# The second pair of a recursive up-projection made classical, its operand differences moved to later pairs

## The chip, the cores and the metric

The kernel runs on 1 core of a Trainium2 chip. The metric is the device time of one execution in microseconds. Times inside an execution are read from one profiled execution and count from the start of its span.

## The reference

One decoder block over 2048 tokens of 1024 channels, in float32. The part that the change touches is the gated MLP:

```
v    = rms_norm(h, g_ffn)
up   = causal_dwconv(v @ w_up, w_conv_ffn, b_conv_ffn)      # 1024 -> 2 x 3072, three taps
gate, val = up[..., :3072], up[..., 3072:]
h    = h + (gelu(gate) * val) @ w_down                      # 3072 -> 1024
```

Ahead of it stand an input projection with a linear recurrence and a causal pooling, and an output projection; behind it a gated per-layer embedding (`w_ple_gate`, `w_ple_proj`) and a last RMS norm.

## The kernel before

Everything is stored channel-major: a tile is 128 channels on the partitions by tokens. The tokens are done in two blocks of 1024, one after the other, each through all stages: mixing, output projection, eight products of the embedding (`pp`), the MLP, the gate of the embedding.

**Precision.** A float32 operand is split in two parts, hi = the rounded value and lo = the remainder, and a product of two such operands is three matmuls: hi x hi, hi x lo, lo x hi. Weights come in panels of 4 tiles of 128x128 (`raw`, a ring of 5 buffers, loaded by SP's queue). ScalarE writes the panel's hi part (`hi(n)`, L627), VectorE the lo part (`lo(n)`, L1069), in rings of 4 (`whi`, `wlo`). `hi(n)` waits until TensorE has used panel n - 4, and for TensorE a panel is ready when `lo(n)` is done. A raw buffer is loaded again when its last panel's `lo` is done.

**The MLP.** The 3072 channels of gate and val are 24 tiles each. Tile q of gate and tile q of val are a pair. Pair 0 of each block is done classically: 8 input tiles, each times gate's and val's weights, times two halves of 512 tokens, times three = 96 matmuls, with gate and val interleaved tile by tile, as the input's splits become ready. Every other pair is one level of Strassen's recursion in Winograd's form: the pair's 2x2 matrix of (gate, val) x (lower, upper half of the input channels) times the input's 2x2 matrix of (channel halves) x (token halves) takes seven products P1 to P7 of 12 matmuls, 84 in all. Its left operands are four panels as they are or sums of panels, which VectorE forms afresh in each pair (`wsummed`, L1065, one buffer). Its right operands are the input's quarters B11, B12, B21, B22 and four differences T1 to T4. They are formed once a block by VectorE (L1321, 128x2048), in place in the input `UN`, and split by ScalarE (L804) and VectorE (L1326). T4's split parts overwrite those of B12.

The products run in the order P1 P5 P6 P3 P7 P2 P4. Between them ScalarE copies partial results out (`snap_p1` after P1, `snap_p5`, `snap_u2`), and VectorE adds others (`c12_out` after P3, `c22_out` after P7, `c11_out` after P2). P6 waits for `snap_p1`, P3 for `snap_p5`, P7 for `snap_u2` and P4 for `c22_out`. In the first recursive pair P5, P6, P7 and P4 also wait for T1, T2, T3 and T4.

Each finished pair is convolved: for gate and for val one ScalarE pass (`gate_sum`, `val_sum`) and two chained VectorE passes (`gate_conv`, `val_conv`), then gelu (ScalarE), a product (`f_tile`) and its split into `f_split` (`f_hi_tile`, `f_lo_tile`). Four pairs make a chunk of f, and after each chunk come the 8 down products (192 matmuls). Results leave in four PSUM slots used in turn.

Each engine's program is a list written out by hand, and an engine works through it strictly in that order; engines meet only in semaphores. For the opening of the stage there are own lists, `first_pair` and `second_pair` on ScalarE and VectorE; from then on `pair(b, q)` is repeated. In `first_pair` the embedding's products are also brought out (`keep_pp`) and the input is normalised and split (`normalised`, `b_hi_tile`, `b_lo_tile`).

Of the kernel before, what the change touches and what calls it, by code (L numbers as in the profile page):

```python
# [36 lines left out]
AHEAD_DOWN = 3  # L37

# [6 lines left out]
PRODUCTS = (("P1", B11), ("P5", T1), ("P6", T2), ("P3", B22), ("P7", T3), ("P2", B21), ("P4", T4))  # L45
OP_AT = {B11: 4, B12: 5, B21: 1, B22: 2, T1: 3, T2: 0, T3: 6, T4: 5}
# [8 lines left out]
def plan():  # L55
# [46 lines left out]
    for b in range(BLOCKS):  # L102
# [83 lines left out]
PAIRS = FT - 1  # L186
# [35 lines left out]
def build(nc, xT, pT, wpan, par_d, outT, pp_d):  # L222
    with ExitStack() as ctx:
# [34 lines left out]
        f_split = place("f_split", [P, 2, CHUNK, BLOCK], F32R, F0)  # L258
# [82 lines left out]
        def landed(r):  # L341
            return panel_in[r % RAW_RING], 16 * (r // RAW_RING + 1)

# [92 lines left out]
        def _(pe):  # L436
# [62 lines left out]
            def first_pair(b):  # L499
                gate, val = (b, "gate", 0), (b, "val", 0)  # L500
                pe.wait_ge(*free(gate))
                pe.wait_ge(*free(val))
                for k in range(DT):
# [7 lines left out]
                    if k % KP == KP - 1:  # L511
                        mm.then_inc(pe_step, 1)
# [13 lines left out]
            def pair(b, q):  # L526
                xy, z = (b, "XY", q), (b, "Z", q)
                s = b * PAIRS + q - 1
                X, Y, Z = psum(xy)[:, 0:BANK], psum(xy)[:, BANK:BLOCK], psum(z)[:, 0:BANK]

                def t_formed(i):
                    if q == 1:
                        pe.wait_ge(t_ready, b * 4 + i)
# [4 lines left out]
                t_formed(1)  # L538
                product(b, q, "P5", T1, Z, True)
                pe.wait_ge(snapped, 3 * s + 1)  # L540
                t_formed(2)
# [4 lines left out]
                t_formed(3)  # L546
# [3 lines left out]
                t_formed(4)  # L550
                product(b, q, "P4", T4, X, False)

            def down(b, c, m, k0, k1):
# [5 lines left out]
                for k in range(k0, k1):  # L559
                    pe.wait_ge(f_ready, b * FT + c * CHUNK + k + 1)  # L560
                    mm = tile_products(psum(key), n, k,
                                       lambda part, h, k=k: f_split[:, part, k, h * BANK:(h + 1) * BANK],
# [5 lines left out]
            for b in range(BLOCKS):  # L568
# [23 lines left out]
                for c in range(CHUNKS):  # L592
                    for q in range(c * CHUNK, (c + 1) * CHUNK):
                        if q == 0:
                            first_pair(b)
                        else:
                            pair(b, q)
# [21 lines left out]
        def _(act):  # L619
# [181 lines left out]
            def t_hi_half(b, i, name):  # L801
                act.wait_ge(t_sum, b * 4 + i)
                half = {T1: (0, 0), T3: (0, 1), T2: (1, 1), T4: (1, 0)}[name]
                nc.scalar.activation(op_half(name, 0), un_half(*half), ACT.Copy).then_inc(t_hi, 1)  # L804
# [9 lines left out]
            def gate_sum(b, q):  # L814
                if q:
                    act.wait_ge(*out_of((b, "Z", q)))
                    act.wait_ge(c11, b * PAIRS + q)
# [807 lines left out]
```

## Time and profile before

| | us |
|---|---|
| median of 3 runs | 2225.94 (2224.36 to 2226.24) |
| the profiled execution | 2225.44 |
| its span, first to last instruction | 2223.7 |
| TensorE busy | 2159.3 (97%) |
| VectorE busy | 1545.0 (69%) |
| ScalarE busy | 1025.2 (46%) |
| mean granted TensorE clock | 0.990 |

A granted clock of 1.00 is 2.4 GHz and 0.50 is 1.2 GHz. The difference between the profiled execution's time and its span, 1.7 us, lies outside the first and the last instruction. In the timeline rows one row may merge several instructions of a kind (x2, x4); a row's duration is longer than the distance from its start to the next start, as instructions of an engine overlap at their ends.

### The profile page before, as it was taken

What the parts mean: (1) busy time and instruction counts of PE and PEld (TensorE: products, weight loads), DVE (VectorE), ACT (ScalarE), POOL (GpSimd) and SP (SyncE); (2) the same over time, 40 slices, a digit from 0 to 9 for tenths busy, and PEclk for the clock granted to TensorE, in tenths of its full rate; (3) what the DMA queues carried; (4) which work ended last, traced back from release to release, by engine and by line L of the source; (5) the groups of instructions that cost most, each with busy time, mean ns of one, the idle gap of its engine ahead of it and who ended that gap; (6) DMA issues with size and microseconds to landing.
All of it is one profiled execution on the core that took longest, in us unless ns stands there. A gap on an engine that the chain in (4) does not pass through costs nothing.

```text
span 2223.7 us, 24264 instructions
## 1 busy us (share of the span) xinstructions
PE 2159.3 (97%) x9416; PEld 1775.3 (80%) x9416; DVE 1545.0 (69%) x1769; ACT 1025.2 (46%) x1403; POOL 0.2 (0%) x4
## 2 busy tenths in 40 slices
PE   8999989999999999999999999899999999999995
PEld 6877868888888888888888788688888888888884
DVE  7884497585858575777888736967667575848765
ACT  5763455352525253454555625534334352525443
POOL 0000000000000000000000000000000000000000
PEclk9999999999999999999999999999999999999998
DMA  3114211121211111133221233111211121211222
GB/s 142 51 43 152 95 57 57 41 73 38 67 40 54 50 57 57 51 134 106 70 114 50 71 126 114 38 57 43 72 38 63 43 66 38 72 43 53 71 100 76
DMA packets 73154, 154.81 MB, mean 70 GB/s; under 512 B 7888, under 2 KB 8016, under 8 KB 73040
## 3 DMA queue, kind: packets, MB, share of 16 engines
q1 hardware_dynamic: 70736, 144.87, 19.4%
q10 hardware_dynamic: 2304, 8.39, 0.9%
q8 instruction: 75, 1.23, 0.2%
q14 instruction: 39, 0.32, 0.0%
HBM read 136.45 MB, written 16.78 MB: 69 GB/s over the span
## 4 chain that ended last, share of the span: by engine, by line
PE 90%; DVE 6%; ACT 2%; issue 1%; DMA 0%; SPq 0%; ACTq 0%; DVEq 0%
PE slot L448 51%; PE slot L521 38%; DVE wlo L1069 1%; DVE UN L1309 1%; DVE ops L1314 1%; DVE UN L1321 1%; DVE H L1538 0%; DMA XN<-xT 0%; DVE H L1268 0%; PE slot L477 0%; ACT ops L804 0%; DVE ops L1326 0%; ACT whi L627 0%; DVE H L1264 0%; DVE H L1274 0%
## 5 line engine op out<-in xcount | busy, mean ns | idle before, releaser
L521 PE MATMUL slot<-ops,whi 128*128 128x512 f32 x2576 | 799.2, 392 | 19.3 <-ACT WG L853 9.9
L521 PEld LDWEIGHTS slot<-ops,whi 128*128 128x128 f32 x2576 | 486.5, 189 | 123.4 <-ACT WG L853 10.7
L521 PE MATMUL slot<-ops,wlo 128*128 128x512 f32 x1288 | 503.5, 391 | 0.0
L627 ACT ACTIVATE whi<-raw 128x512 fp32r<-128x512 f32 x370 | 229.1, 625 | 469.1 <-PE slot L448 312.1
L448 PE MATMUL slot<-f_split,whi 128*128 128x512 f32 x1536 | 410.5, 389 | 0.0
L448 PEld LDWEIGHTS slot<-f_split,whi 128*128 128x128 f32 x1536 | 288.4, 188 | 59.8
L1069 DVE TENSOR_TENSOR wlo<-raw,whi 128x512 fp32r<-128x512 f32 x370 | 249.5, 687 | 60.8 <-ACT whi L627 60.0
L521 PEld LDWEIGHTS slot<-ops,wlo 128*128 128x128 f32 x1288 | 243.3, 189 | 50.9
L627 ACT ACTIVATE whi<-wsum 128x512 fp32r<-128x512 f32 x184 | 115.6, 628 | 322.7 <-DVE wsum L1065 191.9
L1463 DVE TENSOR_TENSOR H<-slot,H 128x1024 f32<-128x1024 f32 x96 | 117.3, 1222 | 182.1 <-PE slot L448 182.1
L448 PE MATMUL slot<-f_split,wlo 128*128 128x512 f32 x768 | 236.4, 389 | 0.0
L448 PE MATMUL slot<-Uhi,whi 128*128 128x512 f32 x640 | 202.4, 398 | 17.6 <-DVE wlo L1069 16.9
L448 PE MATMUL slot<-Ulo,whi 128*128 128x512 f32 x640 | 198.5, 392 | 0.0
L448 PE MATMUL slot<-Uhi,wlo 128*128 128x512 f32 x640 | 198.5, 392 | 0.0
L448 PEld LDWEIGHTS slot<-f_split,wlo 128*128 128x128 f32 x768 | 144.2, 188 | 29.9
L1069 DVE TENSOR_TENSOR wlo<-wsum,whi 128x512 fp32r<-128x512 f32 x184 | 126.8, 689 | 51.2 <-ACT whi L627 51.2
L448 PEld LDWEIGHTS slot<-Uhi,whi 128*128 128x128 f32 x640 | 120.9, 190 | 46.9 <-issue 15.5
L448 PEld LDWEIGHTS slot<-Ulo,whi 128*128 128x128 f32 x640 | 121.4, 190 | 25.7
L448 PEld LDWEIGHTS slot<-Uhi,wlo 128*128 128x128 f32 x640 | 121.0, 189 | 25.3
L448 PE MATMUL slot<-Yhi,whi 128*128 128x512 f32 x304 | 93.9, 390 | 3.4 <-DVE Ylo L1278 3.4
L448 PE MATMUL slot<-Yhi,wlo 128*128 128x512 f32 x304 | 93.6, 389 | 0.0
L448 PE MATMUL slot<-Ylo,whi 128*128 128x512 f32 x304 | 93.5, 389 | 0.0
(176 smaller groups left out, 2222.9 us busy)
## 6 DMA issues: line engine op xcount, KB each, us to landing
raw<-panels SPq DMA_DIRECT2D x416, 256.0 KB, 2.7
XN<-xT SPq DMA_DIRECT2D x8, 1024.0 KB, 9.0
H<-xT SPq DMA_DIRECT2D x8, 1024.0 KB, 11.0
pp_kept<-XQ ACTq DMA_DIRECT2D x16, 512.0 KB, 2.6
PPR<-pp_kept SPq DMA_DIRECT2D x16, 512.0 KB, 3.5
outT<-H SPq DMA_DIRECT2D x8, 512.0 KB, 2.7
outT<-H SPq DMA_DIRECT2D x16, 256.0 KB, 2.4
WG<-pT SPq DMA_DIRECT2D x2, 512.0 KB, 9.1
```

The lines of the kernel that those rows point to most:

```text
L448: mm = pe.matmul(ps[:, h * BANK:(h + 1) * BANK], stat_[:, w], mov(part, h), start=first and i == 0, stop=last and i == 2)
L521: mm = pe.matmul(ps, stat_[:, w], (lo if part else hi)[:, k, :], start=first and k == 0 and i == 0, stop=k == KP - 1 and i == 2, skip_grou ...
L627: nc.scalar.activation(whi[n % RING][:], source(n), ACT.Copy).then_inc(panel_hi, 1)
L1069: v.tensor_tensor(wlo[n % RING][:], source(n), f32(whi[n % RING][:]), ALU.subtract).then_inc(panel_lo, 1)
L1309: v.scalar_tensor_tensor(UN[:, k, :], H[:, k, :], col("g_ffn", k), rms_tile(1), ALU.mult, ALU.mult).then_inc(un_ready, 1)
L1314: v.tensor_tensor(b_tile(k, 1), halves(UN[:, k, :]), f32(b_tile(k, 0)), ALU.subtract).then_inc(b_ready, 1)
L1321: v.tensor_tensor(un_half(*dst), un_half(*left), un_half(*right), ALU.subtract).then_inc(t_sum, 1)
L1463: v.tensor_tensor(H[:, m, :], psum(key)[:], H[:, m, :], ALU.add).then_inc(slot_free[SLOT[key]], 1)
```

## The change

Pair 1 of each block is done classically as well, so 22 instead of 23 pairs a block are recursive, and the first recursive pair is pair 2. In pair 1 all of gate (48 matmuls) comes ahead of all of val (48). The four differences are formed in the order T1, T3, T2, T4: T1 and T3 on VectorE behind the last splits of the input, T2 during pair 1, T4 during pair 2, once B12 is no longer used. Their splits, the convolutions and the panels of pairs 0 to 2 stand in new lists (`second_pair`, `third_pair`). `keep_pp(6)`, `keep_pp(7)` and the panel c0 + 3 come a place or two earlier in `first_pair`. `f_split` is laid out tile by tile, so that f's first tiles overwrite the part of `UN` that is free first. The four raw panels of pair 1 are loaded in the order of their use. Counts of semaphores follow (`PAIRS`, `q - CLASSICAL`, `t_count(b, name)` = 4b + the place of the name in the order + 1).

The core of the diff: plan, buffers, TensorE, ScalarE's lists, VectorE's lists.

```diff
-                if q == 0:
+                if q < CLASSICAL:
                     job(b, "gate", q)
                     job(b, "val", q)
-                    for name, i in (("gate", 0), ("val", 0), ("gate", 1), ("val", 1)):
+                    for name, i in ((("gate", 0), ("val", 0), ("gate", 1), ("val", 1)) if q == 0 else
+                                    (("gate", 0), ("gate", 1), ("val", 0), ("val", 1))):
                         panel((b, name, q, i), raw((name, q, i)))
-                    for i in range(2):
-                        step(b, "pair0", i)
+                    for i in range(2 if q == 0 else 0):
+                        step(b, "whole", q, i)
                         for name in ("gate", "val"):
-                            close((b, name, q, i), STEP[b, "pair0", i], (b, "pair0", i))
+                            close((b, name, q, i), STEP[b, "whole", q, i], (b, "whole", q, i))
+                    for name in ("gate", "val") if q else ():
+                        for i in range(2):
+                            step(b, name, q, i)
+                            close((b, name, q, i), STEP[b, name, q, i], (b, name, q, i))
                     continue
...
-        f_split = place("f_split", [P, 2, CHUNK, BLOCK], F32R, F0)
+        f_split = place("f_split", [P, CHUNK, 2, BLOCK], F32R, F0)
...
+            def second_pair(b):
+                for key in ((b, "gate", 1), (b, "val", 1)):
+                    pe.wait_ge(*free(key))
+                    for i in range(2):
+                        n = PANEL[(*key, i)]
+                        pe.wait_ge(panel_lo, n + 1)
+                        for k in range(KP):
+                            mm = tile_products(psum(key), n, k,
+                                               lambda part, h, k=i * KP + k: b_tile(k, part)[:, h, :],
+                                               i == 0 and k == 0, i == 1 and k == KP - 1)
+                        mm.then_inc(pe_step, 1)
...
+            def pair_out(b, q, name, tile):
+                key = (b, name, q)
+                if q:
+                    act.wait_ge(pe_step, STEP[b, name, q, 1])
+                    act.wait_ge(v_conv if name == "val" else g_conv, b * FT + q)
+                else:
+                    act.wait_ge(pe_step, STEP[b, "whole", 0, 1])
+                if b:
+                    halo_in(b, q, name == "val", tile)
+                nc.scalar.activation(tile[:, HALO_FFN:HALO_FFN + BLOCK], psum(key)[:], ACT.Copy
+                                     ).then_inc(slot_free[SLOT[key]], 1)
             def first_pair(b):
                 c0 = PANEL[b, "gate", 0, 0]
-                n0 = PANEL[b, 1, "P1"]
+                c1 = PANEL[b, "gate", 1, 0]
                 keep_pp(b, 0)
                 keep_pp(b, 1)
                 hi(c0)
...
                 keep_pp(b, 5)
                 b_hi_tile(b, 2)
                 hi(c0 + 2)
+                keep_pp(b, 6)
                 b_hi_tile(b, 3)
-                keep_pp(b, 6)
+                keep_pp(b, 7)
                 b_hi_tile(b, 4)
-                keep_pp(b, 7)
+                hi(c0 + 3)
                 load_table(ACT.Gelu_apprx_tanh)
                 b_hi_tile(b, 5)
-                hi(c0 + 3)
                 b_hi_tile(b, 6)
+                hi(c1)
                 b_hi_tile(b, 7)
-                t_hi_half(b, 1, T1)
-                hi(n0)
+                hi(c1 + 1)
                 for i in range(3):
                     act.wait_ge(pp_out[i], 16 * (b + 1) * len(range(i, DT, 3)))
-                t_hi_half(b, 2, T3)
+                t_hi_half(b, T1)
+            def second_pair(b):
+                c1 = PANEL[b, "gate", 1, 0]
+                n0 = PANEL[b, 2, "P1"]
+                pair_out(b, 0, "gate", WG)
+                gate_sum(b, 0)
+                pair_out(b, 0, "val", WV)
+                val_sum(b, 0)
+                hi(c1 + 2)
+                hi(c1 + 3)
+                gelu(b, 0)
+                t_hi_half(b, T3)
+                pair_out(b, 1, "gate", WG)
+                gate_sum(b, 1)
+                hi(n0)
                 hi(n0 + 1)
-                t_hi_half(b, 3, T2)
-                for name, tile in (("gate", WG), ("val", WV)):
-                    key = (b, name, 0)
-                    act.wait_ge(pe_step, STEP[b, "pair0", 1])
-                    if b:
-                        halo_in(b, 0, name == "val", tile)
-                    nc.scalar.activation(tile[:, HALO_FFN:HALO_FFN + BLOCK], psum(key)[:], ACT.Copy
-                                         ).then_inc(slot_free[SLOT[key]], 1)
-                    if name == "gate":
-                        gate_sum(b, 0)
+                t_hi_half(b, T2)
+                act.wait_ge(t_ready, t_count(b, T3))
+                f_hi_tile(b, 0)
+                gelu(b, 1)
+                pair_out(b, 1, "val", WV)
+                val_sum(b, 1)
                 hi(n0 + 2)
-            def second_pair(b):
-                n0 = PANEL[b, 1, "P1"]
-                val_sum(b, 0)
+            def third_pair(b):
+                q = CLASSICAL
+                n0 = PANEL[b, q, "P1"]
+                snap_p1(b, q)
                 hi(n0 + 3)
-                gelu(b, 0)
-                snap_p1(b, 1)
-                snap_p5(b, 1)
-                t_hi_half(b, 4, T4)
+                snap_p5(b, q)
                 hi(n0 + 4)
-                snap_u2(b, 1)
                 hi(n0 + 5)
-                f_hi_tile(b, 0)
+                f_hi_tile(b, q - 1)
+                snap_u2(b, q)
                 hi(n0 + 6)
+                act.wait_ge(pe_step, STEP[b, "val", 1, 1])
+                t_hi_half(b, T4)
                 hi(n0 + 7)
                 hi(n0 + 8)
                 hi(n0 + 9)
-                gate_sum(b, 1)
+                gate_sum(b, q)
...
                     b_lo_tile(b, k - 1)
                     if k == 3:
                         lo(c0 + 2)
-                    if k == 6:
+                    if k == 5:
                         lo(c0 + 3)
                 b_lo_tile(b, DT - 1)
-                t_formed(b, 1, (0, 0), (0, 1), (0, 0))
-                t_formed(b, 2, (0, 1), (1, 1), (0, 1))
+                lo(c1)
+                t_formed(b, T1, (0, 1), (0, 0))
+                lo(c1 + 1)
+                t_formed(b, T3, (1, 1), (0, 1))
+                t_lo_half(b, T1)
+            def second_pair(b):
+                c1 = PANEL[b, "gate", 1, 0]
+                n0 = PANEL[b, 2, "P1"]
+                gate_conv(b, 0)
+                val_conv(b, 0)
+                lo(c1 + 2)
+                lo(c1 + 3)
+                f_tile(b, 0)
+                t_formed(b, T2, (1, 1), (0, 0))
+                t_lo_half(b, T3)
+                wsummed(n0 + 1)
+                gate_conv(b, 1)
                 lo(n0)
-                t_lo_half(b, 1, T1)
-                t_formed(b, 3, (1, 1), (1, 1), (0, 0))
-                wsummed(n0 + 1)
-                t_lo_half(b, 2, T3)
                 lo(n0 + 1)
                 wsummed(n0 + 2)
-                t_lo_half(b, 3, T2)
+                f_lo_tile(b, 0)
+                t_lo_half(b, T2)
                 lo(n0 + 2)
-            def second_pair(b):
-                n0 = PANEL[b, 1, "P1"]
-                gate_conv(b, 0)
+            def third_pair(b):
+                q = CLASSICAL
+                n0 = PANEL[b, q, "P1"]
                 wsummed(n0 + 3)
+                val_conv(b, q - 1)
                 lo(n0 + 3)
-                val_conv(b, 0)
-                t_formed(b, 4, (1, 0), (1, 0), (1, 1))
                 wsummed(n0 + 4)
-                t_lo_half(b, 4, T4)
+                f_tile(b, q - 1)
                 lo(n0 + 4)
-                c12_out(b, 1)
-                f_tile(b, 0)
+                t_formed(b, T4, (1, 0), (1, 1))
                 lo(n0 + 5)
-                f_lo_tile(b, 0)
+                f_lo_tile(b, q - 1)
                 lo(n0 + 6)
+                c12_out(b, q)
+                t_lo_half(b, T4)
                 lo(n0 + 7)
                 wsummed(n0 + 8)
-                c22_out(b, 1)
+                c22_out(b, q)
                 lo(n0 + 8)
                 wsummed(n0 + 9)
-                c11_out(b, 1)
+                c11_out(b, q)
                 lo(n0 + 9)
```

## Rows read from the trace of the kernel before

**Rows 1.** The page: busy time by engine, and the chain's shares by engine.
```profile
PE 2159.3 (97%) x9416; PEld 1775.3 (80%) x9416; DVE 1545.0 (69%) x1769; ACT 1025.2 (46%) x1403; POOL 0.2 (0%) x4
...
PE 90%; DVE 6%; ACT 2%; issue 1%; DMA 0%; SPq 0%; ACTq 0%; DVEq 0%
```

**Rows 2.** The table of TensorE's waits: total us, times, longest us.
```profile
PE slot L521 <- ACT WG L853: 9.9, 2, 5.1
PE slot L521 <- DVE wlo L1069: 8.1, 4, 2.7
```

**Rows 3.** Windows: length, busy us and instructions by engine, granted clock, DMA.
```profile
279.51:301.27 21.76, 21.76 (x98) 18.03 (x96) 21.33 (x18) 13.92 (x15) 0.00 (x0) 1.00 0.25 88
301.27:334.39 33.12, 23.69 (x86) 18.06 (x84) 29.40 (x29) 17.34 (x24) 0.00 (x0) 0.85 0.10 32
334.39:372.47 38.08, 38.08 (x170) 31.55 (x168) 31.83 (x40) 22.46 (x35) 0.00 (x0) 1.00 0.22 71
1393.71:1426.99 33.28, 23.41 (x85) 17.82 (x84) 29.48 (x29) 17.52 (x25) 0.00 (x0) 0.85 0.10 32
```

**Rows 4.** The chain that ended last: start, us, what, with its count.
```profile
416.15 76.16 PE slot L521 x336
```

**Rows 5.** TensorE's timeline: start, duration of the group, idle before it.
```profile
301.27 0.62 PE L521 MATMUL slot<-ops,whi 128*128 128x512 f32 x2
...
306.82 1.19 PE L521 MATMUL slot<-ops,whi 128*128 128x512 f32 x2 [2.67 <-DVE wlo L1069]
...
310.95 0.39 PE L521 MATMUL slot<-ops,wlo 128*128 128x512 f32 x1
316.14 1.22 PE L521 MATMUL slot<-ops,whi 128*128 128x512 f32 x2 [4.80 <-ACT WG L853]
...
320.95 0.62 PE L521 MATMUL slot<-ops,whi 128*128 128x512 f32 x2
...
325.13 0.70 PE L521 MATMUL slot<-ops,whi 128*128 128x512 f32 x2 [1.28 <-DVE wlo L1069]
...
331.53 0.73 PE L521 MATMUL slot<-ops,whi 128*128 128x512 f32 x2 [0.68 <-DVE WV L1363]
...
1399.33 1.19 PE L521 MATMUL slot<-ops,whi 128*128 128x512 f32 x2 [2.74 <-DVE wlo L1069]
```

**Rows 6.** VectorE's timeline in block 0, opening of the feed-forward stage.
```profile
300.98 2.28 DVE L1321 TENSOR_TENSOR UN<-UN 128x2048 f32<-128x2048 f32 x1
303.18 0.68 DVE L1065 TENSOR_TENSOR wsum<-raw,raw 128x512 f32<-128x512 f32 x1
303.79 2.28 DVE L1326 TENSOR_TENSOR ops<-UN,ops 128x2048 fp32r<-128x2048 f32 x1
305.99 0.68 DVE L1069 TENSOR_TENSOR wlo<-wsum,whi 128x512 fp32r<-128x512 f32 x1
306.77 0.69 DVE L1065 TENSOR_TENSOR wsum<-wsum,raw 128x512 f32<-128x512 f32 x1
...
310.74 1.28 DVE L1331 SCALAR_TENSOR_TENSOR AG<-WG,par,AG 128x1024 f32<-128x1024 f32 x1
...
313.25 0.68 DVE L1065 TENSOR_TENSOR wsum<-raw,wsum 128x512 f32<-128x512 f32 x1
...
325.50 1.21 DVE L1346 TENSOR_TENSOR AV<-AG,AV 128x1024 f32<-128x1024 f32 x1
326.63 0.68 DVE L1069 TENSOR_TENSOR wlo<-raw,whi 128x512 fp32r<-128x512 f32 x1
```

**Rows 7.** ScalarE's timeline, the same stretch.
```profile
303.96 0.63 ACT L627 ACTIVATE whi<-wsum 128x512 fp32r<-128x512 f32 x1 [3.93 <-DVE wsum L1065]
...
306.30 1.01 ACT L913 ACTIVATE WG<-slot 128x1024 f32<-128x1024 f32 x1
...
307.43 1.24 ACT L824 ACTIVATE AG<-WG,par 128x1024 f32<-128x1024 f32 x1
308.58 1.00 ACT L913 ACTIVATE WV<-slot 128x1024 f32<-128x1024 f32 x1
```

More of the change, by code:

```diff
@@ L37 @@
 AHEAD_DOWN = 3
+CLASSICAL = 2
 POOL_ORDER = (0, 2, 3, 1)
@@ L561, in down @@
                     mm = tile_products(psum(key), n, k,
-                                       lambda part, h, k=k: f_split[:, part, k, h * BANK:(h + 1) * BANK],
+                                       lambda part, h, k=k: f_split[:, k, part, h * BANK:(h + 1) * BANK],
                                        k == 0, k == KP - 1)
@@ L595, in _ @@
                             first_pair(b)
+                        elif q == 1:
+                            second_pair(b)
                         else:
@@ L799, in b_hi_tile, with t_hi_half @@
                 nc.scalar.activation(b_tile(k, 0), halves(UN[:, k, :]), ACT.Copy).then_inc(b_hi, 1)
[L801 to L804, printed above, removed]
+            def t_hi_half(b, name):
+                act.wait_ge(t_sum, t_count(b, name))
+                nc.scalar.activation(op_half(name, 0), un_half(*T_HALF[name]), ACT.Copy).then_inc(t_hi, 1)
             def halo_in(b, q, stream, tile):
@@ L814, in gate_sum @@
             def gate_sum(b, q):
-                if q:
+                if q >= CLASSICAL:
                     act.wait_ge(*out_of((b, "Z", q)))
-                    act.wait_ge(c11, b * PAIRS + q)
+                    act.wait_ge(c11, b * PAIRS + q - CLASSICAL + 1)
                 else:
-                    act.wait_ge(*out_of((b, "gate", 0)))
+                    act.wait_ge(*out_of((b, "gate", q)))
                 if b + 1 < BLOCKS:
@@ L827, in val_sum @@
             def val_sum(b, q):
-                if q:
+                if q >= CLASSICAL:
                     act.wait_ge(*out_of((b, "XY", q)))
-                    act.wait_ge(c22, b * PAIRS + q)
+                    act.wait_ge(c22, b * PAIRS + q - CLASSICAL + 1)
                 else:
-                    act.wait_ge(*out_of((b, "val", 0)))
+                    act.wait_ge(*out_of((b, "val", q)))
                 if b + 1 < BLOCKS:
@@ L845, in f_hi_tile @@
                 act.wait_ge(f_raw, b * FT + q + 1)
-                nc.scalar.activation(f_split[:, 0, q % CHUNK, :], AV[:, 0:BLOCK], ACT.Copy).then_inc(f_hi, 1)
+                nc.scalar.activation(f_split[:, q % CHUNK, 0, :], AV[:, 0:BLOCK], ACT.Copy).then_inc(f_hi, 1)
             def snap_p1(b, q):
@@ L941, in pair @@
                     c21_out(b, q - 1)
+                if follows:
                     val_sum(b, q - 1)
@@ L963, in ffn @@
                             second_pair(b)
+                        elif q == CLASSICAL:
+                            third_pair(b)
                         else:
@@ L1315, in b_lo_tile, with t_formed, t_lo_half @@
                                 ).then_inc(b_ready, 1)
-            def t_formed(b, i, dst, left, right):
-                if i > 1:
-                    dve.wait_ge(t_sum, b * 4 + i - 1)
-                v.tensor_tensor(un_half(*dst), un_half(*left), un_half(*right), ALU.subtract).then_inc(t_sum, 1)
-            def t_lo_half(b, i, name):
-                dve.wait_ge(t_hi, b * 4 + i)
-                half = {T1: (0, 0), T3: (0, 1), T2: (1, 1), T4: (1, 0)}[name]
-                v.tensor_tensor(op_half(name, 1), un_half(*half), f32(op_half(name, 0)), ALU.subtract
+            def t_formed(b, name, left, right):
+                if name != T_ORDER[0]:
+                    dve.wait_ge(t_sum, t_count(b, name) - 1)
+                v.tensor_tensor(un_half(*T_HALF[name]), un_half(*left), un_half(*right), ALU.subtract
+                                ).then_inc(t_sum, 1)
+            def t_lo_half(b, name):
+                dve.wait_ge(t_hi, t_count(b, name))
+                v.tensor_tensor(op_half(name, 1), un_half(*T_HALF[name]), f32(op_half(name, 0)), ALU.subtract
                                 ).then_inc(t_ready, 1)
@@ L1349, in f_lo_tile @@
                 dve.wait_ge(f_hi, b * FT + q + 1)
-                v.tensor_tensor(f_split[:, 1, q % CHUNK, :], AV[:, 0:BLOCK], f32(f_split[:, 0, q % CHUNK, :]),
+                v.tensor_tensor(f_split[:, q % CHUNK, 1, :], AV[:, 0:BLOCK], f32(f_split[:, q % CHUNK, 0, :]),
                                 ALU.subtract).then_inc(f_ready, 1)
```

30 lines of the change are left out of this document (18 added, 12 removed).

## The prediction

> **What bounds the kernel now.** I read the page first: its busy line has TensorE at 97% of the span, and its chain that ended last lies for 90% on TensorE, 6% on VectorE and 2% on ScalarE [rows 1]. So matmuls set the time, and only two things can change it: the number of matmuls, and the places where TensorE waits. Next the table of waits, for where those places are [rows 2]: the longest wait of a product of the recursive multiplication (L521) is 5.1 us, twice, for ScalarE's copy of P1 at L853; four more of L521 are for a weight remainder (`wlo`). Two or four times in two blocks means once or twice a block, so I asked for windows around pair 1, the first recursive pair [rows 3]. Pair 0 (96 matmuls) takes 21.76 us, pairs 2 and 3 together (168) take 38.08, both gapless at clock 1.00: 0.2267 us a matmul. The chain's row of 336 matmuls in 76.16 us has the same pitch [rows 4]. Pair 1, with 84 matmuls, takes 33.12 us in block 0 and 33.28 in block 1, at a mean clock of 0.85. Gapless it would be 84 x 0.2267 = 19.04. So 14.08 and 14.24 us are lost there, and that is what this change can win.
>
> The matmul timeline shows the loss [rows 5]: idle 2.67 us ahead of P5, 4.80 ahead of P6, 1.28 ahead of P7, 0.68 ahead of P4, and twelve matmuls after the first of these that take 306.82 to 311.18 (the last starts at 310.95) = 4.36 us where 2.72 is normal: 1.64 lost to the lower clock. After the 4.80 gap twelve take 320.95 - 316.14 = 4.81.
> The reason for the gaps is VectorE: 29.40 us busy of 33.12 [rows 3]. Each of the four differences costs it 2.20 us to form and 2.20 to split (start to start, 300.98 to 303.18 and 303.79 to 305.99), each panel 0.61, and the two convolutions 2.51 each [rows 6].
>
> **The matmuls added.** Pair 1 becomes 2 x 8 x 2 x 3 = 96 matmuls instead of 84: 12 more, 2.72 us a block, 5.44 in all, certain. If nothing waited any more, a block would gain 14.08 - 2.72 = 11.36 us (11.52 in block 1), 22.9 in all. This is one end of my range.
> The Trainium skill, "TensorE: Matmul & The Clock Gate", section "Back-to-back issue gap", gives N/2.4 + 2.5 ns, which is 216 ns for these 512 columns, and 131 ns for a sustained stream in a real kernel. By the first the 24 added matmuls would cost an estimated 5.2 us and by the second 3.1; the trace's 226.7 ns disagrees with both, and decides.
>
> **Panels of pair 1.** It needs four raw panels and no sum (three panels and all four sums go). Counting back from the difference at 300.98 [rows 6] over the remainder before it (2.20), a panel (0.6), a wait of some 0.2 and two differences (4.40), VectorE is done with the input's splits at about 293.5. Then lo, T1 formed, lo: both gate panels stand at 296.9, ahead of 301.27. ScalarE evicts pair 0 from 301.5; eviction with halo copy 1.13, sum 1.15 [rows 7], so the gate convolution starts at 303.9, both convolutions end at 308.9 and val's two remainders at 309.6 and 310.2. PE wants them at 301.27 + 48 x 0.2267 = 312.15 and 5.4 later: hidden, by 2.5 us. This cover is what "gate ahead of val" gives; without it the four panels would all be due within 2.72 us. The loads behind these panels go out as each remainder frees its buffer, at the latest at 310, for a use at 316 or later; the moved `keep_pp`, `hi` and table load keep inside TensorE's 21.76 us of pair 0. The new layout of f_split reads the same 512 contiguous columns: nothing.
>
> **The differences, spread.** T1 and T3 fall into pairs 0 and 1, T2 is formed at 311.2 and split by 323.9, after gate_conv(1), two remainders, a sum and f's remainder. P5 wants T1 at 325.75 and P6 wants T2 at 328.47. Those three stalls of before go.
>
> **What is late next.** Pair 1's val ends at 323.03 and must be evicted before pair 2 can go on. ScalarE: 323.03 + 0.2 (my allowance for the handover) + 1.13 + 1.15 + 0.62 for `hi(n0+2)` (0.63 in [rows 7]) = 326.13. VectorE has waited for that since 323.9, and from here it has, in its order, before c22_out is through: lo and its handover to the next sum 0.78 (305.99 to 306.77), sum 0.61, val_conv(1) 2.51, lo 0.78, sum 0.61, f_tile 1.13, lo 0.61, T4 formed 2.20, lo 0.61, f's remainder 1.13, lo 0.61, c12_out 0.61, T4's remainder 2.20, lo 0.61, sum 0.61, c22_out 0.69 = 16.3 [rows 6]. It ends at 342.45, and P4, which waits for c22, starts at 342.5. Gapless it would start after six products, at 323.03 + 6 x 2.72 = 339.35. **So a wait of 3.15 us a block comes back**, some 0.4 of it perhaps ahead of P7 already (snap_u2 stands behind f_hi on ScalarE), the rest, about 2.7 idle, ahead of P4. Queued behind c22_out are two remainders, a sum and c11_out, 2.5 us, done before P4 ends; pair 3 then finds its panels ready, as pair 2 does now. P3 is tight too (remainder at 330.7, wanted at 331.2), but P4's time doesn't depend on it: VectorE's chain is longer.
>
> **The clock after that wait.** An idle of 2.67 us (block 0) and one of 2.74 (block 1) were each followed by matmuls of double pitch (1.19 us for two), one of 1.28 and one of 0.68 were not (0.70 and 0.73) [rows 5]. A wait of 2.7 is nearest to the first two, so I take 1.6 us more a block, with 0 and 2.1 (4.81 - 2.72) as bounds. The Trainium skill, same page, section "Part 1: The HAM clock gate", says that the number of slow matmuls varies from run to run of one kernel. By that the cost is no constant here either: a rival below.
>
> **The sum.** Per block 14.08 - 2.72 - 3.15 - 1.6 = 6.6 us, in block 1 6.8: 13.4 us. The profiled span of 2223.7 becomes 2210.3; the profiled run took 2225.44, so 2212.0, and the runs' median is 0.5 above it: **2212.4 us**. The rest of the 2200 us is untouched: TensorE works from the same buffers, in the same order, after pair 3.
>
> **Rivals.**
> - The clock doesn't fall at P4's wait, or in one block only: 1.6 or 3.2 us less, 2209.2 to 2210.8. For it: 2.7 us idle is no longer than the shortest that showed a fall, and a small part of it may fall ahead of P7. Chance 0.27.
> - VectorE reaches c22 in time (handovers overlap, the order has slack I don't see): up to 3.15 + 1.6 per block less, 2203 to 2208. Against it: 16.3 us of work are counted from starts of rows. 0.07.
> - More waits: val's panels, P3 or P6 late, because ScalarE's queue holds `hi` behind evictions that wait for TensorE. Every microsecond per block costs two, and a second fall of the clock 1.6 more: 2215 to 2221. Margins are 2.5 us (val), 0.5 (P3), 1.5 (P6). 0.14.
> - No gain: the work only moves; what VectorE was late with at pair 1 it is late with at pair 2, c22 slipping by 6.6 us more than forecast. Against it: with 12 matmuls more and a second pair ahead of the first recursive product, VectorE has 38 us where it had 16 to P4. 2221.5 to 2230. 0.04.
> - Slower, by one mechanism: the clock stays low after P4's wait. A matmul at low clock costs (4.81 - 2.72)/12 = 0.17 us or more extra, so 40 more of them a block eat the gain, and a whole slow pair 3 (84) costs 15 us a block, 2240. In the rows it was back within twelve matmuls each time. 0.03.
>
> **Chances and range.** The forecast as it stands (2211 to 2214) has 0.45. Less than 0.2 in all should lie outside 2207 to 2217.5: of the better tail (0.07) most, of the worse ones (0.21) about half. 0.2% is 4.45 us, about what a measurement of this kernel can tell from no change. Faster by more than that (below 2221.5): 0.45 + 0.27 + 0.07 + 0.14 = 0.93; within: 0.04; slower: 0.03.
>
> **What would show it.** In the profile after: no idle between pair 0 and P1 of pair 2 (301 to 323); L521's waits down to P4's, for DVE at c22_out (L1363 of before), of 2 to 3 us, twice, and perhaps a few tenths for snap_u2; matmuls of double pitch after it; chunk 0's down products starting at 365.9 in block 0 instead of 372.47; 24 matmuls more. Wrong: a wait for `wlo` between gate and val of pair 1 (my panel count failed), a wait ahead of P6 (T2 or n0+2), or a P4 that doesn't wait. If the down products start at 364.3, only the clock's term was wrong.

## The result and the profile after

The median is 2212.86 us (2211.46 to 2213.12, four runs) against 2226.05 before: ratio 0.9943, 95% interval 0.9931 to 0.9954. The forecast was 2212.4 in a range of 2207.0 to 2217.5. The profiled execution took 2213.12 us with a span of 2211.3, 12.4 less than before.

Line numbers have moved: tile products are L459 (L448 before), products of the recursion L546 (L521), differences L1375 (L1321), their remainders L1380 (L1326), panel remainders L1123 (L1069), `c22_out` L1417, `snap_u2` L892, `snap_p1` L879. The page of the kernel after, its busy line and its chain's shares, answer to [rows 1]:

```profile
PE 2160.3 (98%) x9440; PEld 1776.8 (80%) x9440; DVE 1531.9 (69%) x1749; ACT 1021.6 (46%) x1393; POOL 0.2 (0%) x4
...
PE 94%; DVE 4%; ACT 1%; DMA 0%; issue 0%; SPq 0%; DVEq 0%; ACTq 0%
```

TensorE has the 24 matmuls more, and its share of the chain grew from 90 to 94%: VectorE, ScalarE and issue gave up what it gained. TensorE's table of waits answers to [rows 2]:

```profile
PE slot L546 <- DVE WV L1417: 4.9, 2, 2.4
...
PE slot L546 <- ACT WG L892: 0.6, 2, 0.3
```

These are all the waits of recursive products that are left: twice 2.4 us for `c22_out`, twice 0.3 for `snap_u2`. The windows answer to [rows 3]; the first four lines are pair 0, pair 1, pair 2 up to P4, and P4 with pair 3; the last two are the same two parts of pairs 2 and 3 in block 1:

```profile
279.98:301.74 21.76, 21.76 (x97) 18.02 (x96) 21.48 (x18) 12.69 (x15) 0.00 (x0) 1.00 0.32 113
301.74:323.50 21.76, 21.76 (x97) 18.02 (x96) 18.91 (x17) 15.66 (x18) 0.00 (x0) 1.00 0.08 24
323.50:343.03 19.53, 16.79 (x74) 13.25 (x72) 17.25 (x18) 10.75 (x15) 0.00 (x0) 1.00 0.19 55
343.03:366.56 23.53, 23.53 (x97) 19.26 (x97) 18.39 (x23) 12.85 (x21) 0.00 (x0) 0.93 0.24 69
1409.60:1429.13 19.53, 16.85 (x74) 13.24 (x72) 17.25 (x18) 10.94 (x17) 0.00 (x0) 1.00 0.17 55
1429.13:1452.62 23.49, 23.49 (x96) 19.27 (x97) 18.34 (x23) 12.77 (x20) 0.00 (x0) 0.93 0.22 70
```

Pair 1 runs gapless in 21.76 us at clock 1.00, where it took 33.12 at 0.85. Pair 2 up to P4 takes 19.53 us, where six gapless products take 16.32: 3.21 of waits. P4 and pair 3 are 96 matmuls, 21.76 us at full clock, and take 23.53 at a mean clock of 0.93: 1.77 lost. I measure all kernels below by one length, **the opening**: from pair 0's first matmul to the first down product. Before it was 92.96 us in block 0 and 93.12 in block 1; after it is 366.56 - 279.98 = 86.58, and 86.54 in block 1. 6.38 + 6.58 = 12.96 us gained. Block 0's opening begins 0.47 us later than before, which leaves 12.5; the span gained 12.4.

TensorE's timeline around P4, in block 0:

```profile
334.86 0.73 PE L546 MATMUL slot<-ops,whi 128*128 128x512 f32 x2 [0.32 <-ACT WG L892]
...
343.03 0.72 PE L546 MATMUL slot<-ops,whi 128*128 128x512 f32 x2 [2.43 <-DVE WV L1417]
...
344.63 1.05 PE L546 MATMUL slot<-ops,whi 128*128 128x512 f32 x2
```

The first matmuls behind the gap are at full pitch (0.72 us for two); those of half the clock (1.05) begin 1.6 us later. In [rows 5] they came first. VectorE's rows show the chain that holds P4:

```profile
322.42 2.29 DVE L1380 TENSOR_TENSOR ops<-UN,ops 128x2048 fp32r<-128x2048 f32 x1
326.66 0.69 DVE L1123 TENSOR_TENSOR wlo<-wsum,whi 128x512 fp32r<-128x512 f32 x1 [1.95 <-ACT whi L654]
...
333.75 2.28 DVE L1375 TENSOR_TENSOR UN<-UN 128x2048 f32<-128x2048 f32 x1
...
338.89 2.28 DVE L1380 TENSOR_TENSOR ops<-UN,ops 128x2048 fp32r<-128x2048 f32 x1
...
342.29 0.68 DVE L1417 TENSOR_TENSOR WV<-slot,WV 128x512 f32<-128x512 f32 x1
```

VectorE idles 1.95 us until ScalarE has written the hi part of panel n0 + 2, which stands on ScalarE behind the copy and the sum of pair 1's val. Then it works without a pause for 16.3 us, T4's two operations among them, to the end of `c22_out` at 342.97. P4 starts 0.06 later.

### The profile page after: what moved, and what is told of

Same layout as the page of the kernel before. It is cut to its first block, busy times and chain, and to the rows that moved or that the text cites. A ratio compares the mean times of both kernels' runs of the same rounds, so it can differ in the third digit from the quotient of the medians.

```text
span 2211.3 us, 24258 instructions
## 1 busy us (share of the span) xinstructions
PE 2160.3 (98%) x9440; PEld 1776.8 (80%) x9440; DVE 1531.9 (69%) x1749; ACT 1021.6 (46%) x1393; POOL 0.2 (0%) x4
## 4 chain that ended last, share of the span: by engine, by line
PE 94%; DVE 4%; ACT 1%; DMA 0%; issue 0%; SPq 0%; DVEq 0%; ACTq 0%
PE slot L459 57%; PE slot L546 37%; DVE wlo L1123 1%; PE slot L488 1%; DMA XN<-xT 0%; DVE H L1608 0%; DVE H L1322 0%; DVE H L1318 0%; DVE H L1328 0%; DVE ops L1380 0%; ACT H L780 0%; DVE UN L1375 0%; DVE wsum L1119 0%; DVE AV L1394 0%; DVE AG L1247 0%
## 5 line engine op out<-in xcount | busy, mean ns | idle before, releaser
L546 PE MATMUL slot<-ops,whi 128*128 128x512 f32 x2464 | 761.4, 390 | 5.4 <-DVE WV L1417 4.9
L546 PEld LDWEIGHTS slot<-ops,whi 128*128 128x128 f32 x2464 | 463.7, 188 | 103.5 <-DVE WV L1417 5.7
L546 PE MATMUL slot<-ops,wlo 128*128 128x512 f32 x1232 | 480.6, 390 | 0.0
L459 PE MATMUL slot<-f_split,whi 128*128 128x512 f32 x1536 | 410.5, 389 | 0.0
L459 PEld LDWEIGHTS slot<-f_split,whi 128*128 128x128 f32 x1536 | 288.3, 188 | 59.9
L1123 DVE TENSOR_TENSOR wlo<-raw,whi 128x512 fp32r<-128x512 f32 x372 | 251.0, 687 | 60.1 <-ACT whi L654 59.2
L546 PEld LDWEIGHTS slot<-ops,wlo 128*128 128x128 f32 x1232 | 232.0, 188 | 48.5
L654 ACT ACTIVATE whi<-wsum 128x512 fp32r<-128x512 f32 x176 | 110.6, 629 | 307.8 <-DVE wsum L1119 183.5
L459 PE MATMUL slot<-f_split,wlo 128*128 128x512 f32 x768 | 236.4, 389 | 0.0
L459 PE MATMUL slot<-Uhi,whi 128*128 128x512 f32 x640 | 201.8, 397 | 18.1 <-DVE wlo L1123 17.2
L459 PE MATMUL slot<-Ulo,whi 128*128 128x512 f32 x640 | 198.8, 392 | 0.0
L459 PE MATMUL slot<-Uhi,wlo 128*128 128x512 f32 x640 | 198.7, 392 | 0.0
L459 PEld LDWEIGHTS slot<-f_split,wlo 128*128 128x128 f32 x768 | 144.1, 188 | 29.9
L459 PEld LDWEIGHTS slot<-Uhi,whi 128*128 128x128 f32 x640 | 120.8, 190 | 47.6 <-issue 16.1
L1123 DVE TENSOR_TENSOR wlo<-wsum,whi 128x512 fp32r<-128x512 f32 x176 | 121.3, 689 | 52.8 <-ACT whi L654 52.8
L459 PEld LDWEIGHTS slot<-Ulo,whi 128*128 128x128 f32 x640 | 121.2, 189 | 25.6
L459 PEld LDWEIGHTS slot<-Uhi,wlo 128*128 128x128 f32 x640 | 121.1, 189 | 25.4
L459 PE MATMUL slot<-Yhi,whi 128*128 128x512 f32 x304 | 93.9, 390 | 3.4 <-DVE Ylo L1332 3.4
L459 PE MATMUL slot<-Yhi,wlo 128*128 128x512 f32 x304 | 93.6, 389 | 0.0
L459 PE MATMUL slot<-Ylo,whi 128*128 128x512 f32 x304 | 93.6, 389 | 0.0
## 6 DMA issues: line engine op xcount, KB each, us to landing
H<-xT SPq DMA_DIRECT2D x8, 1024.0 KB, 10.9
```

What stands on the lines that cost most here:

```text
L459: mm = pe.matmul(ps[:, h * BANK:(h + 1) * BANK], stat_[:, w], mov(part, h), start=first and i == 0, stop=last and i == 2)
L546: mm = pe.matmul(ps, stat_[:, w], (lo if part else hi)[:, k, :], start=first and k == 0 and i == 0, stop=k == KP - 1 and i == 2, skip_grou ...
L654: nc.scalar.activation(whi[n % RING][:], source(n), ACT.Copy).then_inc(panel_hi, 1)
L1123: v.tensor_tensor(wlo[n % RING][:], source(n), f32(whi[n % RING][:]), ALU.subtract).then_inc(panel_lo, 1)
```

## The experiments

All medians stand beside runs of the kernel before on the same chip: 2225.78 us for the first four experiments, 2224.24 for the three behind them, 2225.98 for the last three kernels. Opening lengths are from the profiled executions. The "changed kernel" is the kernel after. Differences between the medians of two variants also hold up to 3.6 us from other stages (experiment 8); the opening lengths hold none of that.

**1. T4 formed early.** In the changed kernel, VectorE's lists: out of `third_pair`, into `second_pair`.

```diff
                 t_lo_half(b, T2)
+                t_formed(b, T4, (1, 0), (1, 1))
                 lo(n0 + 2)
...
                 lo(n0 + 4)
-                t_formed(b, T4, (1, 0), (1, 1))
                 lo(n0 + 5)
```

> T4 is formed two places earlier, in the 1.95 us in which VectorE waits for ScalarE ahead of the remainder of panel n0 + 2 (in the changed kernel that remainder starts at 326.66). My theory: P4 waits because VectorE's chain from the eviction of pair 1's val to c22_out is full; with 2.20 us taken out of it and 0.25 of them given back where the idle time was too short, c22_out ends 1.95 us earlier, P4's idle falls from 2.43 to about 0.5 us, and with a gap that short the clock stays at 1.00, so the 1.77 us of slow matmuls go too: 3.7 us a block, 7.4 in all, 2205.5 us. Rival 1 (something else than VectorE's chain holds P4, such as its panel): no change, 2212.9. Rival 2 (the slow matmuls have another cause than the gap): only 1.95 a block, 2209.0.

Measured: 2205.12 us, ratio 0.9907 (0.9894 to 0.9921); openings 83.38 and 83.39 us, 3.2 less than after. TensorE and VectorE:

```profile
333.64 0.73 PE L546 MATMUL slot<-ops,whi 128*128 128x512 f32 x2 [0.41 <-ACT WG L892]
340.10 0.73 PE L546 MATMUL slot<-ops,whi 128*128 128x512 f32 x2 [0.72 <-DVE WV L1417]
```

```profile
323.25 2.28 DVE L1375 TENSOR_TENSOR UN<-UN 128x2048 f32<-128x2048 f32 x1
325.45 0.68 DVE L1123 TENSOR_TENSOR wlo<-wsum,whi 128x512 fp32r<-128x512 f32 x1
...
335.94 2.29 DVE L1380 TENSOR_TENSOR ops<-UN,ops 128x2048 fp32r<-128x2048 f32 x1 [0.38 <-ACT ops L830]
```

Forming T4 fills the idle time, and P4 starts 340.10 - (278.62 + 43.52) = 17.96 us behind pair 2's start instead of 19.53. 1.57 instead of 1.95 came of it, because a new wait of 0.38 us for ScalarE's part of T4 stands in VectorE's chain. The clock is 1.00 over the whole opening, in both blocks. Both rivals fell: VectorE's chain holds P4, and with the gap at 0.72 us the slow matmuls are gone. A block gained 3.2 us for 3.7 expected. The median fell by 7.7 us, of which the two openings explain 6.4.

**2. c22_out ahead of two panel operations**, in the changed kernel:

```diff
                 t_lo_half(b, T4)
+                c22_out(b, q)
                 lo(n0 + 7)
                 wsummed(n0 + 8)
-                c22_out(b, q)
```

> c22_out goes ahead of the remainder of panel n0 + 7 and the sum of panel n0 + 8 in VectorE's list of pair 2. My theory: c22_out comes 2 x 0.60 = 1.2 us earlier, P4's idle falls from 2.43 to 1.2 us; gaps of 1.28 and 1.37 us left the clock at 1.00 in the kernel before, so the slow matmuls go as well: 3.0 us a block, 2207.0 us in all. Rival (the clock falls also after this gap): 1.2 a block, 2210.5.

Measured: 2209.05 us, ratio 0.9925 (0.9911 to 0.9938); openings 85.39 and 85.45, 1.2 less than after. The clock behind it is 1.00, but TensorE has a new wait, in the next pair:

```profile
341.81 0.74 PE L546 MATMUL slot<-ops,whi 128*128 128x512 f32 x2 [1.21 <-DVE WV L1417]
351.60 0.74 PE L546 MATMUL slot<-ops,whi 128*128 128x512 f32 x2 [1.33 <-ACT WG L879]
```

P4 starts 1.2 us earlier as expected, and P6 of pair 3 now waits 1.33 for `snap_p1`, which stands behind the gelu of pair 2 on ScalarE and with it behind VectorE's `gate_conv(2)`. TensorE would reach P6 3.0 us earlier than in the changed kernel, 1.2 by P4 and 1.8 by the clock, and VectorE's work was only put in another order. That order even costs VectorE 0.6 us: the sum of panel n0 + 8 now comes behind `c22_out`, ScalarE's hi part of it comes later too, and VectorE stands idle for it. The first row is the changed kernel, the second this one:

```profile
343.13 0.69 DVE L1123 TENSOR_TENSOR wlo<-wsum,whi 128x512 fp32r<-128x512 f32 x1 [0.16 <-ACT whi L654]
343.72 0.69 DVE L1123 TENSOR_TENSOR wlo<-wsum,whi 128x512 fp32r<-128x512 f32 x1 [0.76 <-ACT whi L654]
```

Neither text had this wait. I had looked only as far as P4.

**3. Both edits.**

> Both of the former edits. My theory: c22_out would come 3.15 us earlier than in the changed kernel, P4's wait of 2.8 us goes entirely (c22_out then waits for P7 or is just in time), the clock stays; 4.3 to 4.6 us a block, 2203.7 to 2204.3 us, some 0.3 us ahead of P7 are left. Rival (the first edit already takes P4's wait to nothing measurable): the same time as with the first edit alone, within 1 us.

Measured: 2205.19 us, ratio 0.991 (0.9896 to 0.9923); openings 83.80 and 83.89, 0.4 to 0.5 longer than with the first edit alone. The theory's 2203.7 to 2204.3 us was missed: P4's wait is gone, but P6 of pair 3 waits 1.14 and 1.24 us for `snap_p1`. The time agrees with the rival's, for another reason than it gave: the same load of VectorE is met at pair 3's P6.

**4. Filler matmuls in P4's wait**, in the changed kernel, ahead of the wait for `c22_out`:

```diff
+                if q == CLASSICAL:
+                    pe.wait_ge(panel_lo, PANEL[b, q, "P4"] + 1)
+                    for _ in range(10):
+                        pe.matmul(psum(z)[:, BANK:BLOCK], whi[PANEL[b, q, "P4"] % RING][:, 0:P],
+                                  op_half(B21, 0)[:, 0, :], start=True, stop=True)
                 pe.wait_ge(c22, s + 1)
```

> The changed kernel with ten matmuls more in each block, ahead of P4's wait for c22_out; they multiply a tile of B21 by a weight tile into the unused second half of Z's PSUM slot, and nothing reads their result. They take 2.27 us of the 2.8 that TensorE waits there, so P4 starts when it did. Theory (the doubled pitch of P4's later matmuls comes from TensorE's idle time ahead of it): the clock stays at 1.00, 1.77 us a block less, 3.5 in all: 2209.3 us, with P4 starting at the same distance from pair 2's start, 19.5 us. Rival (it comes from something else, such as the work of the other engines or the wait itself): no change, 2212.9, and the slow matmuls are still there.

Measured: 2207.97 us, ratio 0.992 (0.9907 to 0.9934); openings 84.97 and 84.95, 1.6 less than after.

```profile
340.11 2.43 PE L577 MATMUL slot<-ops,whi 128*128 128x512 f32 x10
342.70 0.74 PE L546 MATMUL slot<-ops,whi 128*128 128x512 f32 x2 [0.17 <-DVE WV L1422]
```

P4 starts at 342.70, again 19.5 us behind pair 2's start (279.66 + 43.52 = 323.18), so the wait for VectorE is untouched, and 20 useless matmuls make the kernel faster. The clock term was the idle time's doing, in this kernel: 1.6 us a block. The clock fell in all six openings profiled without the filler (experiment 8) and in neither of the two with it. The median fell by 4.9 us, more than the 3.2 of the openings.

**5. Panels of pair 1 interleaved**: gate's first, val's first, gate's second, val's second, in the plan and on TensorE.

```diff
-                for key in ((b, "gate", 1), (b, "val", 1)):
-                    pe.wait_ge(*free(key))
-                    for i in range(2):
+                for i in range(2):
+                    for key in ((b, "gate", 1), (b, "val", 1)):
+                        if i == 0:
+                            pe.wait_ge(*free(key))
```

> Pair 1 classical as in the changed kernel, but gate and val interleaved half by half of the input channels: gate's first panel, val's first, gate's second, val's second. Both now end together, 21.76 us after the start. The text of the prediction said that all four panels would then be due within 2.72 us; counted again from the plan, two panels are due at the start (ready at 297.3) and one after 10.9 and one after 16.3 us, as before, so no wait for panels is to be expected. What changes is that gate can't be evicted at half time: eviction, sum and convolution of gate (1.13 + 1.15 + 2.51 us) move behind the end of pair 1 and ahead of val's. Theory: c22_out and with it P4 come 4 to 5 us later a block (VectorE idle in pair 1, overloaded in pair 2), and P6 or P3 wait too: 2221 to 2226 us. Rival (VectorE has room): within 1 us of 2212.9. Rival (panels are the cover, as the prediction said): waits for a weight remainder within pair 1.

Measured: 2211.84 us, ratio 0.9943 (0.993 to 0.9957); openings 86.84 in both blocks. Its waits in block 0:

```profile
323.90 0.70 PE L546 MATMUL slot<-ops,whi 128*128 128x512 f32 x2 [0.38 <-DVE wlo L1123]
333.15 0.73 PE L546 MATMUL slot<-ops,whi 128*128 128x512 f32 x2 [0.84 <-ACT WV L887]
336.59 0.73 PE L546 MATMUL slot<-ops,whi 128*128 128x512 f32 x2 [0.44 <-ACT WG L892]
344.76 0.72 PE L546 MATMUL slot<-ops,whi 128*128 128x512 f32 x2 [2.42 <-DVE WV L1417]
```

The theory, 2221 to 2226 us, was some 10 us too slow, and wrong in two ways. Gate and val do not end together: gate's last panel is the third of four, so gate comes out 5.4 us later, not 10.9, and P4 is later by 344.76 - 323.35 - 19.53 = 1.9 us, not 4 to 5. And the clock did not fall behind the same gap. The window from P4 to the down products:

```profile
344.76:366.67 21.91, 21.91 (x96) 18.13 (x97) 18.00 (x23) 12.87 (x21) 0.00 (x0) 1.00 0.25 74
```

21.91 us against 23.53 hides most of the 1.9: the openings are only 0.3 longer. Where the 1.9 comes from, VectorE's row shows: it stands idle for 3.85 us ahead of the convolution of pair 1's gate, which in the changed kernel started without a wait, and the 1.95 of that kernel's later idle time are gone: 3.85 - 1.95 = 1.9.

```profile
320.54 1.28 DVE L1385 SCALAR_TENSOR_TENSOR AG<-WG,par,AG 128x1024 f32<-128x1024 f32 x1 [3.85 <-ACT AG L850]
```

No wait for a weight remainder stands within pair 1 (the 0.38 is pair 2's first).

**6. T2 not spread**: formed and split ahead of the convolutions of pair 0, T3 split there as well.

```diff
                 t_lo_half(b, T1)
+                t_formed(b, T2, (1, 1), (0, 0))
+                t_lo_half(b, T3)
+                t_lo_half(b, T2)
```

(the three stand later in the changed kernel; ScalarE's parts move likewise)

> The changed kernel with T2 not spread: it is formed behind T3, and T3 and T2 are split ahead of the convolutions of pair 0. VectorE stands idle for 2.66 us there, so 6.60 - 2.66 = 3.9 us of delay for both convolutions and for the remainders of val's panels, which end 4 us later: the first at 314.0 instead of 310.1, wanted at 312.6. Theory: a wait for a weight remainder of about 1.5 us at val of pair 1, in each block; what was taken out of pair 1 (6.6 us) lets VectorE catch up before val's end, and from there the times are as they were, shifted by 1.5: 2215.9 us, more by up to 1.8 a block if the clock falls. Rival (VectorE catches up and ScalarE's order hides it): 2212.9. Rival (T2's place doesn't matter for pair 1 but frees VectorE in pair 2): faster than 2212.9.

Measured: 2212.69 us, ratio 0.9946 (0.9931 to 0.9962); openings 88.03 and 86.61.

```profile
313.83 1.16 PE L459 MATMUL slot<-ops,whi 128*128 128x512 f32 x4 [1.32 <-DVE wlo L1123]
...
344.31 1.22 PE L546 MATMUL slot<-ops,whi 128*128 128x512 f32 x2 [2.44 <-DVE WV L1417]
```

```profile
344.31:367.74 23.43, 23.43 (x97) 19.25 (x97) 18.24 (x23) 12.90 (x21) 0.00 (x0) 0.93 0.24 69
1430.38:1452.30 21.92, 21.92 (x97) 18.13 (x98) 18.11 (x23) 12.77 (x20) 0.00 (x0) 1.00 0.23 74
```

The wait at val is there, 1.32 and 1.38 us for 1.5 forecast, and P4 waits as before. Counted from the place where pair 2 would start without a wait, 43.52 us behind pair 0's start, P4 starts after 21.08 us in block 0 and 21.17 in block 1, for 19.53 in the changed kernel: 1.55 and 1.64 later. Block 0's opening is longer by 1.45. Block 1's is longer by only 0.07, since the clock did not fall there. So T2's place in pair 1 is worth 1.6 us a block. The total hardly shows it, and the 2215.9 us expected did not come: the shift was passed on as expected, but this profile was also 1.6 us faster between the two openings (experiment 8).

**7. The layout of f_split alone**, on the kernel before.

> The kernel before with the new layout of f_split alone. Theory: the same contiguous reads and writes at other addresses, no effect: 2226.0, within 0.5 us. Rival (the placement in memory moves matmuls or the writes): the matmul pitch of the down products or the durations of the splits of f differ, and the time by more than 2 us.

Measured: 2225.91 us, ratio 1.0004 (0.9995 to 1.0013): no effect on the time. The trace differs from that of the kernel before in the clock:

```profile
316.71 1.22 PE L521 MATMUL slot<-ops,whi 128*128 128x512 f32 x2 [6.33 <-ACT WG L853]
325.69 0.70 PE L521 MATMUL slot<-ops,whi 128*128 128x512 f32 x2 [1.88 <-DVE wlo L1069]
```

Behind P5's gap of 2.67 us the clock stayed up, and P6's wait grew from 4.80 to 6.33 us; P6 starts 36.64 us behind pair 0's start, for 36.63 in the kernel before. So the slow matmuls of the kernel before cost nothing here: the wait behind them was longer than what they lost.

**8. The changed kernel profiled twice more.**

> The changed kernel once more, nothing edited. P4's wait of 2.43 us comes back in both blocks, at 19.5 us behind the start of pair 2. The question is the clock behind it: in the first profile it fell in both blocks, while with gate and val interleaved the same idle time of 2.42 and 2.44 us was followed by no slow matmul in either. Theory (it falls or not by chance, execution by execution): this look may show 0, 1 or 2 falls, and pair 0's start to the first down product is 84.9 us without and 86.6 us with a fall. Rival (it is a fixed property of this kernel): 86.6 in both blocks again.

> The same once more, for the same question: 84.9 us from pair 0's start to the first down product in a block without a fall of the clock, 86.6 in one with it; the rival expects 86.6 four times in these two looks.

Measured: 2209.50 and 2209.57 us; openings 86.51, 86.57, 86.52 and 86.53. All four openings are of the kind with a fall. The two windows behind P4's start, from the first of the two executions:

```profile
341.09:364.56 23.47, 23.47 (x97) 19.30 (x98) 18.24 (x23) 12.89 (x21) 0.00 (x0) 0.93 0.22 69
1425.51:1449.04 23.53, 23.53 (x96) 19.30 (x97) 18.35 (x23) 12.74 (x20) 0.00 (x0) 0.93 0.24 69
```

So my theory of chance got no support at P4 of this kernel: six of six. But these executions are 3.6 us faster than the first profile with the same openings: 1.9 us ahead of block 0's opening and 1.6 between the openings. There the same kernel does show it. Both profiles have a gap of the same length in the mixing stage, near 159 us; the clock fell behind it in the first profile (the first two rows: the matmuls behind the gap, and the window from there) and not in this one (the last two):

```profile
158.90 0.73 PE L459 MATMUL slot<-Uhi,whi 128*128 128x512 f32 x2 [2.41 <-DVE wlo L1123]
158.40:177.00 18.60, 16.88 (x66) 13.44 (x66) 15.43 (x16) 13.47 (x17) 0.00 (x0) 0.91 0.05 14
158.55 0.74 PE L459 MATMUL slot<-Uhi,whi 128*128 128x512 f32 x2 [2.40 <-DVE wlo L1123]
158.40:177.00 18.60, 16.76 (x72) 13.55 (x73) 16.61 (x18) 13.12 (x16) 0.00 (x0) 1.00 0.04 14
```

In block 1's mixing stage it is the same: 0.90 in the first profile and 1.00 in this one over 1239 to 1256 us, behind gaps of 2.42 us. From the end of block 0's opening to the start of block 1's it is 999.5 us in the profiles of the kernel before, of the changed kernel's first execution and of experiment 2, and 997.9 in all others. That is why medians of variants are not compared by a microsecond or two here. The kernel before and the changed kernel's first profile both have the two falls in the mixing stages, so 12.4 us between them is the change.

**9. Interleaved panels and T4 early**, the edits of 5 and 1 together.

> Pair 1 with its panels interleaved, and T4 formed early as in the first experiment. Interleaving alone left the time as it was (2211.8), but in its profile P4 starts 1.9 us later behind pair 2's start than in the changed kernel, and its clock didn't fall where that of the changed kernel did, which hid 1.8 us. With T4 formed early both sides are free of a long gap. Theory (gate ahead of val is worth about 2 us a block, because gate is brought out 5.4 us earlier): 2205.1 + 2 x 2 = 2209 us, and 85.3 us instead of 83.4 from pair 0's start to the down products. Rival (the order within pair 1 is worth nothing): 2205.1.

Measured: 2212.62 us, ratio 0.994 (0.9923 to 0.9956); openings 87.32 and 87.31.

```profile
323.66 0.70 PE L546 MATMUL slot<-ops,whi 128*128 128x512 f32 x2 [0.38 <-DVE wlo L1123]
331.19 0.70 PE L546 MATMUL slot<-ops,whi 128*128 128x512 f32 x2 [1.81 <-DVE wlo L1123]
345.00 0.73 PE L546 MATMUL slot<-ops,whi 128*128 128x512 f32 x2 [0.72 <-DVE WV L1417]
```

Forming T4 early made this kernel no faster: when gate comes out late, VectorE's idle time lies ahead of gate's convolution (3.85 us, as in experiment 5), and none is left where T4 is now formed, so the 2.20 us push the next remainder back, and P6 waits 1.81. In block 0 the clock fell behind that gap (0.88 over the 13.81 us up to P4), in block 1 behind 1.82 it did not. P4 starts 21.9 us behind the place of pair 2's start in both: its wait for VectorE took in what the slow matmuls lost. Against the first experiment, which differs only in the order of pair 1's panels, the openings are 3.9 us longer each and the median is 7.5 us higher: with T4 early, that is what gate ahead of val is worth, twice what I expected.

## Why the prediction was right

- **The matmuls added**, 2.72 us a block: pair 1 took 21.76 us. Right.
- **What could be won**, 14.08 and 14.24: pair 1 is gapless. Right. Of the 14.08, the 1.64 that the prediction put to the low clock ahead of P6 was no loss of its own: experiment 7 did not have it, and P6 started at the same place. The total is not touched by that. The share of the two parts of the change was not separated but for T2 (1.6 us a block, experiment 6). Keeping pair 1 recursive with the differences spread was not tried.
- **What is late next**, 3.15 us a block up to P4: 3.21 measured (19.53 - 16.32), in both blocks, 0.32 and 0.25 of it idle ahead of P7 and 2.43 and 2.44 ahead of P4 (forecast 0.4 and 2.7); the rest is the slower start of the matmuls behind each gap. VectorE's sum of 16.3 us came out at 342.97 - 326.66 = 16.3. Experiments 1 to 3 show that this chain is the cause.
- **The clock**, 1.6 us a block: 1.77 and 1.73 here, and 1.6 by experiment 4. The size and the cause, idle time, are shown. That it came in both blocks was in part luck: the rule that I used, a gap near 2.7 us is followed by a fall, does not hold in experiments 5 and 6, where the same gap as here had no fall in three blocks of four.
- **The sum**, 13.4 us: 12.96 over the two openings (6.38 = 14.08 - 2.72 - 3.21 - 1.77), 13.2 between the medians. That the median came within 0.5 us of the forecast was luck as well: the prediction took the rest of the kernel as untouched, and there the changed kernel's time moved by 3.6 us from one execution to another, for the most part by the clock (experiment 8).
- **Wrong in the text**: "This cover is what 'gate ahead of val' gives; without it the four panels would all be due within 2.72 us". Interleaved, the panels were due as before and no wait arose within pair 1. What the order gives is an early way out for gate, so that VectorE convolves it while TensorE works on val: 1.9 us a block (experiment 5), 3.9 with T4 early (experiment 9). It did not enter the sum as a term of its own. "P3 is tight" was harmless, as said.
- **The rivals**: more waits, no gain and a lasting low clock did not come; nor did the clock stay up in any of six openings of the changed kernel.

The fastest version is the first experiment's, at 2205.1 us (the third's, 2205.2, is the same within the noise): 0.9907 of the time of the kernel before, against 0.9943. Its gain over the changed kernel is 6.4 us by the openings.

## What to carry to other kernels

When a stall goes, write down for the engine that caused it every instruction from the last one that it must wait for to the one that releases the next product, and sum the distances between starts. Here that sum, 16.3 us, gave the place and size of the new wait before it was seen. Then carry the same sum one product further: moving an instruction within a full list (experiment 2) moves the wait, and only moving work into idle time of that engine (experiment 1) takes most of the wait away, while the same move where there is no idle time buys nothing (experiment 9). And compare variants by the place where the awaited product starts, with the granted clock of the stretches beside it. Interleaving looked free at 2211.8 us, and its openings looked nearly free too (86.84 us against 86.58), because a clock that stayed up hid most of 1.9 us a block; P4's start showed it.

## What the runs showed of the hardware

The granted clock did not follow from the length of the idle time ahead of a matmul. Behind 2.43 and 2.44 us in the changed kernel it fell in six openings of six (mean 0.93 over the next 23.5 us); behind 2.42 and 2.44 in experiment 5 it stayed at 1.00 in both, and in experiment 6 it fell in block 0 and not in block 1. In the kernel before, a gap of 2.67 us was followed by clock 0.50; in experiment 7, the same kernel but for the layout, the clock of 1.00 was held behind the same 2.67 us:

```profile
307.00:308.00 1.00, 0.62 (x3) 1.00 0.00 0
308.00:309.00 1.00, 1.00 (x6) 1.00 0.00 0
309.00:310.00 1.00, 1.00 (x7) 1.00 0.00 0
```

In the changed kernel's mixing stage gaps of 2.40 to 2.42 us did both, in different executions. Nor does the clock always fall at the gap itself. In block 0 of the changed kernel's first profile it fell when TensorE had been at work again for more than a microsecond:

```profile
343.00:344.00 1.00, 0.97 (x4) 1.00 0.00 0
344.00:345.00 1.00, 1.00 (x4) 0.69 0.00 0
345.00:346.00 1.00, 1.00 (x4) 0.50 0.00 0
```

In the second profile of the same kernel the first matmuls behind the same gap were slow already:

```profile
341.09 1.22 PE L546 MATMUL slot<-ops,whi 128*128 128x512 f32 x2 [2.44 <-DVE WV L1417]
```

Gaps of 0.7 to 1.4 us (experiments 1 and 2, and [rows 5]) were followed by no slow matmul in the product behind them. Between these and 2.4 us both occur: behind 1.88 us in block 0 of experiment 7 and 1.81 in block 0 of experiment 9 the clock fell within two microseconds of the restart, behind 1.82 in block 1 of experiment 9 it did not. What decides for gaps of 1.8 to 2.7 us stays open; a forecast should carry it as a term with a chance, here 0 or 1.7 us each time, and as 0 where a longer wait for another engine follows, as at P6 in experiment 7.
